# Row maxima of the first two attentions: subtracted inside the product with the keys' remainder instead of by a product of their own

## The reference

```python
def masked_softmax(s, mask):
    s = jnp.where(mask, s.astype(jnp.float32), -jnp.inf)
    m = jnp.max(s, axis=-1, keepdims=True)
    e = jnp.exp(s - jnp.where(jnp.isfinite(m), m, 0.0))
    return e / jnp.maximum(jnp.sum(e, axis=-1, keepdims=True), 1e-30)

p_slc = masked_softmax(jnp.einsum('bcgrd,bcgnd->bcgrn', qc, kg_sel) * scale, m_slc)
p_win = masked_softmax(jnp.einsum('bcgrd,bkgd->bcgrk', qc, kwc) * scale, m_win)
p = masked_softmax(s_own, m_own).astype(v.dtype)
```

## Time and profile before

| | us |
|---|---|
| median of 3 runs (892.92 to 893.14) | 892.94 |
| the profiled execution, its own time | 895.99 |
| its span in the profile | 894.2 |
| PE busy | 868.4 (97%) |
| DVE busy | 612.5 (68%) |
| ACT busy | 494.7 (55%) |
| POOL busy | 174.6 (20%) |
| PE's share of the chain that ended last | 88% |

### The profile page before, as it was taken

How to read it: one execution, slowest core, us unless ns; L and a number is a source line. 1 busy time by engine, 2 the same in 40 slices (tenths; PEclk the granted TensorE clock), 3 DMA queues, 4 the chain that set the end, 5 groups by cost and what they waited for, 6 DMA issues and landing times.

```text
span 894.2 us, 14775 instructions
## 1 busy us (share of the span) xinstructions
PE 868.4 (97%) x5801; PEld 790.8 (88%) x5801; DVE 612.5 (68%) x976; ACT 494.7 (55%) x780; POOL 174.6 (20%) x189
## 2 busy tenths in 40 slices
PE   3899999999999999999999999999999999999998
PEld 3788899988688889999998888899999899999886
DVE  5875678877877687666665546597668666666552
ACT  3543768555657656544444546677765654444431
POOL 1016345565054520000000004271000000000000
PEclk9999999999999999999999999999999999999999
DMA  9966646456572665666666556553345566666650
GB/s 354 361 203 220 212 147 208 142 162 192 165 240 90 191 198 155 202 200 198 197 192 194 166 155 200 145 162 118 99 139 171 181 195 188 186 188 183 207 176 24
DMA packets 45844, 163.38 MB, mean 183 GB/s; under 512 B 5200, under 2 KB 5584, under 8 KB 45776
## 3 DMA queue, kind: packets, MB, share of 16 engines
q1 hardware_dynamic: 45776, 162.44, 57.4%
HBM read 161.37 MB, written 1.05 MB: 182 GB/s over the span
## 4 chain that ended last, share of the span: by engine, by line
PE 88%; DVE 5%; ACT 3%; DMA 2%; issue 1%; SPq 0%; POOL 0%; DVEq 0%; ACTq 0%
PE bank L518 36%; PE bank L506 34%; PE bank L533 3%; PE bank L703 2%; PE bank L865 2%; PE bank L680 2%; DVE w_lo L1673 1%; DMA x<-in_x 1%; PE bank L705 1%; PE bank L656 1%; DMA w_raw<-in_weights 1%; PE bank L613 1%; PE bank L684 1%; PE bank L759 1%; PE bank L707 1%
## 5 line engine op out<-in xcount | busy, mean ns | idle before, releaser
L1105 ACT ACTIVATE w_hi<-w_raw 128x1024 fp32r<-128x1024 f32 (+2 forms) x249 | 259.5, 1049 | 226.5 <-PE bank L518 121.1
L1673 DVE TENSOR_TENSOR w_lo<-w_raw,w_hi 128x1024 fp32r<-128x1024 f32 (+2 forms) x249 | 301.4, 1221 | 77.5 <-ACT w_hi L1105 76.9
L518 PE MATMUL bank<-h_hi,w_hi 128*128 128x256 f32 x904 | 254.6, 282 | 0.0
L518 PE MATMUL bank<-h_lo,w_hi 128*128 128x256 f32 x904 | 251.8, 279 | 0.0
L518 PE MATMUL bank<-h_hi,w_lo 128*128 128x256 f32 x904 | 251.8, 279 | 0.0
L518 PEld LDWEIGHTS bank<-h_lo,w_hi 128*128 128x128 f32 x904 | 171.4, 190 | 0.5 <-issue 0.2
L518 PEld LDWEIGHTS bank<-h_hi,w_hi 128*128 128x128 f32 x904 | 169.9, 188 | 1.0 <-issue 0.5
L518 PEld LDWEIGHTS bank<-h_hi,w_lo 128*128 128x128 f32 x904 | 169.8, 188 | 0.0
L506 PE MATMUL bank<-w_hi,h_hi 128*128 128x512 f32 (+1 forms) x240 | 96.5, 402 | 2.6 <-DVE w_lo L1673 1.9
L2548 POOL TENSOR_TENSOR ada_acc<-ada_acc,w_raw 128x512 f32<-128x512 f32 x56 | 82.2, 1468 | 68.3 <-ACT w_raw L1109 63.2
L506 PE MATMUL bank<-w_lo,h_hi 128*128 128x512 f32 (+1 forms) x240 | 94.0, 392 | 0.0
(11 more groups left out here) (321 smaller groups left out, 1404.5 us busy)
## 6 DMA issues: line engine op xcount, KB each, us to landing
w_raw<-in_weights SPq DMA_DIRECT2D x298, 512.0 KB, 4.3
w_raw<-in_weights SPq DMA_DIRECT2D x4, 360.0 KB, 3.6
x<-in_x SPq DMA_DIRECT2D x1, 1024.0 KB, 9.7
gate_row<-in_gate_bias SPq DMA_DIRECT2D x2, 512.0 KB, 6.9
out<-x SPq DMA_DIRECT2D x4, 256.0 KB, 3.4
w_raw<-in_weights SPq DMA_DIRECT2D x3, 256.0 KB, 2.6
const<-in_constants SPq DMA_DIRECT2D x1, 285.5 KB, 7.1
cols<-in_columns SPq DMA_DIRECT2D x1, 208.5 KB, 2.6
```

The source lines that it names most:

```text
L518: mm = e.matmul(o, ws[p], xs[q], start=(k + kk == 0 and i == 0 and b % 2 == 0), stop=(k + kk == kts - 1 and i == 2 and (b % 2 == 1 or b == ...
L1105: e.activation(w_hi[i % NSPLIT][:, 0:c], raw[v % NRAW][:, 0:c], ACT.Copy).then_inc(*rounded(v))
L1673: e.tensor_tensor(w_lo[i % NSPLIT][:, 0:c], raw[v % NRAW][:, 0:c], w_hi[i % NSPLIT][:, 0:c].bitcast(F32), ALU.subtract).then_inc(*rested(v))
```

## The change

`minus_r`, `shifts`, `shift`, `first_shifts` and the product of L684 go. Instead the zeros of `kl` carry the subtraction:

- `kl` now has the keys' remainder in partitions 0 to 63 for all groups (so DVE's `k_rests` writes there for both halves), and in partitions 64 to 127 it holds -1 or 0 (POOL memsets): for NSA, -1 in 64 to 95 for the first branch and in 96 to 127 for the second; for MoBA -1 in all 64.
- A new operand takes the place of `qs` in that product: `qm_first` (heads 0 to 3, in the place of the diagonals, where the keys' tokens lie before) and `qm` (all heads; it lies over `h_hi` and `h_lo`, so that it can be written only when the last product of `z1` has read them). Their partitions 0 to 63 get the queries' rounded part by DMA from `qs` (`double`, six DMAs per block: two of 128 KB for heads 0 to 3, two of 128 KB for heads 4 to 7, two of 256 KB for heads 8 to 15), placed on SP's queue between fetches of weights. Their partitions 64 to 127 get diagonals of 32 (NSA, two branches) or 64 (MoBA) queries with the maxima (`spread_maxima` on DVE, for four heads at a time).
- `spread_maxima` is 8 instructions of 32 partitions x 256 elements for four heads of NSA and 2 of 64 x 512 for four heads of MoBA. It stands on DVE in the third step of `z1` and then in NSA's slots 0, 2 and 4 and MoBA's slots 0, 1 and 2.

```diff
-                w.wait_ge(*(shift_done if i else shift_first).at((s, i, x)))
+                for at in (kl_signed.at(s), doubled[min(ha // 4, 2)].at((s, 1)), mx_spread.at((s, ha // 4))):
+                    w.wait_ge(*at)
...
-                    for m, k in enumerate((kh, kl)):
-                        e.matmul(o, k[:, g, br, j * P:(j + 1) * P], qs[:, ha:hb + 1:2, j * P:S], start=m == 0, stop=False,
-                                 skip_group_check=True)
+                    for m, (k, q) in enumerate(((kh, qs[:, ha:hb + 1:2, j * P:S]),
+                                                (kl, doubles_of(ha)[:, 0:3:2, j * P:S]))):
+                        e.matmul(o, k[:, g, br, j * P:(j + 1) * P], q, start=m == 0, stop=False, skip_group_check=True)
                     e.matmul(o[:, :, 0:P], mask_r[:, :], bcast(unit_r[:, :].unsqueeze(1), [P, 2, P]), start=False,
-                             stop=False, skip_group_check=True)
-                    e.matmul(o, minus_r[:, :], shifts[x][:, :, j:TT, :].rearrange("p a t q -> p a (t q)"), start=False,
                              stop=True, skip_group_check=True).then_inc(*scored((s, i, x, j)))
...
+            def spread_maxima(s, g):
+
+                w.wait_ge(*m_reduced.at(last_filling(s, 4 * g + 3)))
+                if g:
+                    w.wait_ge(*streamed.at((of[f"{s}_z1"][-1], 1)))
+                rows_ = 32 if s == "nsa" else 64
+                for i in range(P // rows_):
+                    here = slice(rows_ * i, rows_ * i + rows_)
+                    for br in range(2 if s == "nsa" else 1):
+                        there = slice(HD + rows_ * br, HD + rows_ * br + rows_)
+                        o = doubles_of(4 * g)[there, 0:4, :].rearrange("p h (t c) -> p t h c", t=TT)[:, :, :, here]
+                        e.tensor_tensor(o, bcast(ident[here, here].unsqueeze(1).unsqueeze(1), [rows_, TT, 4, rows_]),
+                                        bcast(mx_read[here, :, 4 * g:4 * g + 4, br].unsqueeze(3), [rows_, TT, 4, rows_]),
+                                        ALU.mult).then_inc(*mx_spread((s, g)))
...
-                    for x_ in range(2 if i + 1 < n else 0):
-                        shift(i + 1, x_)
+                    if s == "nsa" and i in (0, 2, 4):
+                        spread_maxima(s, i // 2 + 1)
+                    if s == "moba" and i < 3:
+                        spread_maxima(s, i + 1)
...
                     z_products("nsa_z0", 0, 0, 1)
+                if j == 2:
+                    spread_maxima("nsa", 0)
                 if j < 3:
                     maxima("nsa", 12 + 2 * j, 13 + 2 * j)
...
+            def double(s, part):
+
+                w.wait_ge(*heads_rounded.at((f"{s}_q{part // 2}", 1 if part else 0, 1)))
+                if part:
+                    w.wait_ge(*streamed.at((of[f"{s}_z1"][-1], 1)))
+                else:
+                    w.wait_ge(*heads_turned.at(("nsa_kskw", 1) if s == "nsa" else ("moba_kv", 0)))
+                for i, here in enumerate(HALVES):
+                    a, b = (i, 4) if part == 0 else (4 + i, 8) if part == 1 else (8 + i, NH)
+                    dst = qm if part else qm_first
+                    e.dma_start(dst[0:HD, a:b:2, :].bitcast(F32), qs[here, a:b:2, :].bitcast(F32)).then_inc(
+                        *doubled[part]((s, i)))
...
-            for u in range(of["moba_z0"][0], len(units)):
+            first, rest = of["moba_z1"][0] + 7, of["moba_z1"][-1] + 8
+            for u in range(of["moba_z0"][0], first):
+                fetch(u)
+            double("moba", 0)
+            for u in range(first, rest):
+                fetch(u)
+            double("moba", 1)
+            double("moba", 2)
+            for u in range(rest, len(units)):
                 fetch(u)
```

More of the change, by code:

```diff
@@ L232, in program @@
         ada_acc = [sb(f"ada_acc{i}", [P, 512]) for i in range(2)]
-        unit_r, minus_r, mask_r = (sb(n, [P, P], F32R) for n in ("unit_r", "minus_r", "mask_r"))
+        unit_r, mask_r = (sb(n, [P, P], F32R) for n in ("unit_r", "mask_r"))
         col = lambda n: cols[:, COLS[n][0]:COLS[n][1]]
@@ L276, in program @@
         keys.close()
-        shifts = [sb(f"shifts{x_}", [P, 2, TT, P], F32R, on=mix) for x_ in range(2)]
+        qm_first = sb("qm_first", [P, 4, S], F32R, on=mix)
         pc_t = zs[:, 8:8 + NKV, :]
```

57 lines of the change are left out of this document (31 added, 26 removed).

## The result

| | before | after |
|---|---|---|
| median of the runs, us | 892.93 (892.38 to 893.14) | 906.08 (904.97 to 907.8) |
| the profiled execution's span | 894.2 | 906.0 |
| PE busy | 868.4 | 867.9 |
| DVE busy | 612.5 | 623.8 |
| mean granted clock of PE | 0.998 | 0.991 |

The change makes the kernel slower: ratio 1.0145, interval 1.0126 to 1.0165, or 13.15 us where 1.65 were forecast. 906.08 lies outside the range.

What follows compares the result with a forecast made beforehand. PE, busy 97% of the span, was taken as the bound, with DVE next. -8.4 + 2.75 + 3.7 + 1.6 + 1.6 + 0.4 = +1.65 us gave 897.6 profiled, 894.6 as median; range 889.0 to 897.2.

Steps and rivals of the forecast that it cites:

- The removed products: PE in both attentions: 0.35 us less per item, 5.6 us for NSA and 2.8 for MoBA, together -8.4 us.
- PE's clock: PE in both attentions: granted clock read as 1.00, the upper level of 2.4 GHz, throughout; no term in the sum.
- Start: Ahead of NSA's first scores: DVE's first block delays the last two maxima, +2.75 us (+2.4 to +4.9).
- Slots 2 and 3: NSA: slot 2's block meets three POOL adds, PE waits for gate row and eviction, +3.7 us (0 to 4.9).
- Slots 4 and 5: NSA: slot 4's block meets POOL's three adds, the column behind it delays PE's second transposes, +1.6 us (0 to 2.8).
- MoBA held back: MoBA's slots: DVE is the bound, so 1.6 us of the 2.8 removed are held back (0 to 2.4).
- Copies: MoBA's slot 1: query copies land at 302.1 to 302.8 for a need at 302.4, +0.4 us (0 to 3).
- Rival 1: NSA's slots 2 and 4: POOL and DVE miss each other, both collision terms vanish, -3.65 us, 889.3 us; chance 0.25.
- Rival 4: MoBA's copies land late, PE waits 3 us, 897.2 us; or blocks cost 0.60 an instruction, 897 and above; chance 0.15.
- slower: Whole kernel: time over 894.7 us, made of nearly half of (3), and Rival 4; chance 0.37.
- (3): NSA's slots 2 and 4: both blocks collide with POOL's adds as forecast, 894.6 us (893.2 to 896.5); chance 0.35.

Runs made afterwards that it cites:

- the last kernel: Changed kernel; NSA's first block on POOL, second ending slot 0, POOL's column 6 to 8 adds held behind blocks, MoBA's three later blocks in slot 0: 893.24 us (1.0009).
- MoBA alone: Changed kernel with NSA's old diagonals and product back, MoBA's first block behind the second maxima group, its other three in slot 0: 895.56 us (1.0028).
- adds_held_moba_early: Changed kernel with POOL's adds for columns 7 and 8 held behind NSA's blocks of slots 2 and 4, MoBA's other three blocks in slot 0: 897.56 us (1.0048).

## Why the prediction was wrong

- **The removed products, -8.4 us: right.** Items without a wait come about 0.35 us closer (MoBA's slot 2: 7.48 to 7.14 us behind).
- **PE's clock: the step that is missing.** The text read the clock as 1.00 throughout and took it as given, so the low clock is a term put at nothing. It was a result of PE's never waiting. Each forecast wait should have carried a second term for the slow stretch behind it: 3 to 4 us over the kernel (the kernel with PE never idle), 2.0 us behind the start's block when that stands alone.
- **Start, +2.75 forecast, 5.1 measured.** The mechanism was right: the wait has the last maxima as releaser, 3.9 us where "near 3" was said. The mis-sized term is the instruction: "I take 0.33, since the count per partition is what sets these two rows apart". It measured 0.45 from start to start (3.56 us for 8), each 0.42 long, so the next did not start before the last had ended. Memory does not set this apart: the diagonals of 128x512 of the earlier trace rows have both inputs in SBUF too, and the second starts 0.60 us behind the first, which lasts 0.68; and in the kernel before a pair of 256 elements that reads PSUM advances by 0.45 where each works on the other half of the partitions:

```profile
614.33 0.88 DVE L1901 TENSOR_TENSOR o_lo<-bank,o_hi 64x256 fp32r<-64x256 f32 x2 [3.00 <-ACT o_hi L1109]
```

  What this pair shares with the new blocks is that each instruction reads or writes other partitions than the one before it. That this is the cause was not tried by itself. The formula of the Trainium skill (VectorE: DVE Perf Modes, the TRN2 errata) made an estimate of 0.42 us for one and 3.4 us for a block without overlap, which the forecast quoted and set aside; the trace agrees with it (0.42 and 3.56). Another 1.1 us came from one of DVE's remainders ahead of it, which met an add (2.31 us, 1.22 in the profile before), although the text allowed only for less interruption there.
- **Slots 2 and 3, +3.7 forecast.** Right in kind and size: block 6.09 us (6.35), three adds, PE waits for the gate row (2.81) and then for the eviction (0.29). The stretch costs 6.2 us plus the 0.7 that two items give back, because 7 us of half clock follow. The waits, 3.1 us, are inside the bound of 4.9; with the clock behind them the stretch is not. The 1.2 us that an add was to cost were 1.0.
- **Slots 4 and 5, +1.6 forecast: right.** 1.28 us of wait, 1.5 us lost beside the item's gain.
- **MoBA held back, +1.6 forecast, the largest miss: the wrong step was "MoBA's pairs become pairs of 64x512, nothing gained or lost".** Without adds the pair takes 1.41 us (before 1.28), but its readers changed: before, slot 3's first item waited for the first of two instructions; now either item needs both, and these, beside adds, take 3.42 us:

```profile
320.90 3.42 DVE L1820 TENSOR_TENSOR qm<-const,mx 64x512 fp32r<-64x512 f32 x2
```

  PE waits 2.2 us (2.4 lost) and then runs at half clock (2.0). The block in `z1`, said to lie in DVE's waits, took 3.38 us beside adds and put off the fillings (0.8 us of wait).
- **Copies, +0.4 forecast:** 0.8 us of wait. They were issued at 305.07, right behind the fetches of 304.17, and MoBA's took 5.0 to 6.5 us instead of the 4.3 of the fetches; NSA's took 2.3 to 4.0.
- **The chances.** Rival 1 (no collision, 889.3 us) did not happen by itself, and the gain of 3.65 us that it promised was not to be had by placing alone: with hardly a collision left in NSA the last kernel gives 893.24, since the evictions behind a block of 3.6 us, ACT's exponentials, the copies and the maxima keep PE standing for about 5.9 us from 140 to 335 us, where it was 0.3 before (waits that both kernels have are not counted). Rival 4 named the copies and dear instructions, and would have allowed "897 and above", but the range was closed at 897.2; no rival had the clock. The chance of "slower" is also added wrongly: nearly half of (3) and (4) make 0.32, not 0.37.

Counted without the 8.4 us of gain, the profile's 13.7 us are 22.1 us of cost, where the forecast had 10.05. By the starts, with 0.35 us added for each item: 6.7 up to slot 1's second item (forecast 2.75), 7.8 from there to the end of the NSA block (5.3), and 7.6 for MoBA with the fillings ahead of it (2.0). The experiments give the same order of size at each place, in kernels of their own, so they need not add up: the first block alone costs 8.0 us between the medians and 6.9 in the profile, the adds held back in slots 2 and 4 give back 8.2 between the medians, and MoBA's blocks moved to slot 0 give back 5.1 in the profile.

## What to carry to other kernels

Work taken from an engine at 97% by giving many small instructions to one at 79% is worth only what stands behind no one: ask of each block who is queued behind it and who waits for that, and hold the other engine's rows back where they would meet it. A wait of a busy PE is to be priced twice, once for itself and once for the slow stretch that can follow. Take an instruction's duration, and what the next one adds, from a row of the same form, with its partitions, and not only with its element count; where there is none, carry the dearer value as a rival of its own.

## What the runs showed of the hardware

- A DVE instruction with two SBUF inputs that meets a POOL add of 1.27 us ends about 1 us later, whatever its own length: 0.42 becomes 1.38 to 1.40 us. Each instruction of a row can meet one: eight small ones took 3.56 us alone, 6.09 with three adds, 9.37 with six.
- The low clock followed every wait of PE of 2.2 us and more in the attentions, for 4 to 16 us; shorter ones were followed by it sometimes (2.0 us with the block on POOL: yes; 2.0 us in MoBA alone: no; 1.28 us in the change's slot 5: no; 0.9 us in the profile of `adds_held_moba_early`, 0.69 from 180 to 185 us: yes). The same kernel differed by up to 10.6 us between executions when it had such waits; that the fall's length differs from one to the next makes them differ is argued from the profiles, which show one execution each.
- POOL makes a 32x256 product in 0.61 us where DVE takes 0.42, and 8 of them, each waiting for the last, in 6.39 us including one collision.
- Alike DVE instructions in a row on all 128 partitions can start before the last has ended (0.60 us from start to start at 0.68 us each). Those on 32 or 64 partitions, each reading or writing others than the one before, did not: 0.43 to 0.45 at 0.42 for 256 elements, both from SBUF and from PSUM, and 0.72 at 0.69 for 64x512. What the cause is was not tried.
- A copy of 128 or 256 KB from SBUF to SBUF landed 2.3 us after its issue at best; MoBA's four in a row behind fetches of weights took 5.0 to 6.5 us in the change and up to 9.2 in `all_moved`.
